# Hybrid decoder trunk on one core: the squares' round trip through memory moves from SyncE's to ScalarE's queue

## What is computed

```python
def _sqrelu_mlp(x, w1, w2):
    h = jax.nn.relu(x @ w1)      # w1: 2048 x 8192
    return (h * h) @ w2          # w2: 8192 x 2048
x = _layer_norm(DEEPNORM_ALPHA * x + y, ln_g[layer, 0], ln_b[layer, 0])
x = _layer_norm(DEEPNORM_ALPHA * x + _sqrelu_mlp(x, mlp_w1[layer], mlp_w2[layer]), ...)
```

## Time and profile before

| | |
|---|---|
| median of 3 runs | 2109.48 us |
| lowest, highest | 2108.84, 2110.66 us |
| the profiled execution | 2110.28 us |
| its span, first to last instruction | 2108.5 us |
| TensorE busy | 99% of the span |
| VectorE busy | 62% |
| ScalarE busy | 46% |
| memory traffic over the span | 208 GB/s |

### The profile page before, as it was taken

How to read it: one execution, slowest core, us unless ns; L and a number is a source line. 1 busy time by engine, 2 the same in 40 slices (tenths; PEclk the granted TensorE clock), 3 DMA queues, 4 the chain that set the end, 5 groups by cost and what they waited for, 6 DMA issues and landing times.

```text
span 2108.5 us, 28846 instructions
## 1 busy us (share of the span) xinstructions
PE 2091.5 (99%) x9914; PEld 1751.4 (83%) x9914; DVE 1316.9 (62%) x1246; ACT 975.1 (46%) x1140; POOL 21.3 (1%) x16
## 2 busy tenths in 40 slices
PE   9999999999999999999999999999999999999999
PEld 7898888888888888888988888888888888878887
DVE  5869666765655565565766666576755645555565
ACT  5596454443443443443644445354434434443442
POOL 0000010000000000000000000010000000000000
PEclk9999999999999999999999999999999999999999
DMA  7665757766766776675554556658766866766773
GB/s 243 190 204 187 238 180 250 248 201 197 242 219 184 242 229 195 204 253 166 190 187 161 164 169 228 201 191 255 233 199 203 256 198 190 250 198 225 241 229 100
DMA packets 249924, 439.68 MB, mean 209 GB/s; under 512 B 15056, under 2 KB 54224, under 8 KB 248816
## 3 DMA queue, kind: packets, MB, share of 16 engines
q1 hardware_dynamic: 248416, 432.79, 64.7%
q10 hardware_dynamic: 1424, 5.77, 0.7%
HBM read 419.63 MB, written 18.87 MB: 208 GB/s over the span
## 4 chain that ended last, share of the span: by engine, by line
PE 88%; DMA 4%; DVE 3%; issue 2%; ACT 2%; SPq 1%; ACTq 0%; DVEq 0%
PE ps L422 68%; PE ps L414 8%; PE ps L411 4%; DMA f<-sq_by_quad 2%; PE ps L707 1%; PE ps L706 1%; PE ps L705 1%; DMA sq_by_quad<-f 1%; DVE wl L992 1%; DVE gate L1066 1%; DMA wst<-in_rg_w_in_dram 1%; SPq L313 1%; ACT wh L738 1%; PE ps L552 1%; DVE f L1322 0%
## 5 line engine op out<-in xcount | busy, mean ns | idle before, releaser
L992 DVE TENSOR_TENSOR wl<-wst,wh 128x1024 fp32r<-128x1024 f32 x743 | 890.7, 1220 | 336.7 <-ACT wh L738 332.1
L738 ACT ACTIVATE wh<-wst 128x1024 fp32r<-128x1024 f32 x743 | 772.0, 1058 | 656.5 <-PE ps L422 416.1
L422 PE MATMUL ps<-wh,hid 128*128 128x512 f32 x2560 | 697.9, 390 | 5.9 <-DVE hid L1304 5.9
L422 PEld LDWEIGHTS ps<-wh,hid 128*128 128x128 f32 x2560 | 479.7, 188 | 107.9 <-issue 6.6
L422 PE MATMUL ps<-wh,xin 128*128 128x512 f32 x2048 | 548.9, 389 | 0.0
L422 PEld LDWEIGHTS ps<-wh,xin 128*128 128x128 f32 x2048 | 384.0, 188 | 79.3
L422 PE MATMUL ps<-wl,hid 128*128 128x512 f32 x1280 | 405.2, 390 | 0.0
L414 PE MATMUL ps<-xin,wh 128*128 128x512 f32 x960 | 332.4, 397 | 1.9 <-DVE wl L992 1.1
L422 PE MATMUL ps<-wl,xin 128*128 128x512 f32 x1024 | 315.2, 389 | 0.0
L422 PEld LDWEIGHTS ps<-wl,hid 128*128 128x128 f32 x1280 | 240.6, 188 | 50.2
L411 PE MATMUL ps<-xin,wl 128*128 128x256 f32 x960 | 257.3, 278 | 0.0
(11 more groups left out here) (138 smaller groups left out, 835.9 us busy)
## 6 DMA issues: line engine op xcount, KB each, us to landing
wst<-in_mlp_w_dram SPq DMA_DIRECT2D x512, 512.0 KB, 4.1
wst<-in_moba_w_qkv_dram SPq DMA_DIRECT2D x96, 512.0 KB, 4.6
wst<-in_rg_w_in_dram SPq DMA_DIRECT2D x62, 512.0 KB, 4.3
wst<-in_rg_w_out_dram SPq DMA_DIRECT2D x32, 512.0 KB, 4.7
sq_by_quad<-f SPq DMA_DIRECT2D x128, 128.0 KB, 2.9
f<-sq_by_quad SPq DMA_DIRECT2D x32, 512.0 KB, 5.1
wst<-in_moba_w_out_dram SPq DMA_DIRECT2D x32, 512.0 KB, 4.5
f<-in_x_dram SPq DMA_DIRECT2D x8, 256.0 KB, 6.3
```

The costliest lines, as they stand in the source:

```text
L422: return pe.matmul(banks(half)[:, a, :], src[:, c, part, a * P:(a + 1) * P], (wl if low else wh)[:, s, w], start=(c == 0 and part + low == 0),
L738: act.activation(wh[:, off % SPLITS, :], wst[:, slot, :], ACT.Copy).then_inc(wh_done, 1)
L992: dve.tensor_tensor(wl[:, off % SPLITS, :], wst[:, off % STAGE, :], wh[:, off % SPLITS, :], ALU.subtract).then_inc(wl_done, 1)
```

## The change

The two waits and the five DMAs of the squares' round trip go from SyncE's queue to ScalarE's, between the splits 14, 15 and 16. The relu is written in two instructions, one per 128 tokens, each in the order in which the scratch is laid out, so the DMAs out move pieces of 1 KB, and the transpose reads its input in order. The hidden channels come out in plain order, and W2 is loaded in plain order. The square multiplies `sqr` by itself. In the opening pair 1 is transposed before the first turn, and 5 warming matmuls stand first instead of 3.

```diff
-        sqr = f2[:, 0:1024].rearrange("p (a n) -> p a n", a=HALVES)
-        quad = f2[:, 1024:2048].rearrange("p (b n) -> p b n", n=P)
+        sqr = f2[:, 0:1024].rearrange("p (q n) -> p q n", q=GROUP)
+        quad = f2[:, 1024:2048].rearrange("p (i n) -> p i n", i=GROUP)
...
+        to_quad = by_quad.rearrange("(q t) (i n) -> i t q n", q=GROUP, i=GROUP)
...
-                to_quad = by_quad.rearrange("(q t) (a i n) -> i t a q n", q=GROUP, a=HALVES, n=P)
-
-                def squares_out(s, t):
-
-                    sp.wait_ge(psum_free, free + s * (2 * NG) + t + 1)
-                    for i in range(GROUP):
-                        sp.dma_start(to_quad[i], sqr[i * 32:(i + 1) * 32, :, :].rearrange("t a (q n) -> t a q n", n=P))\
-                          .then_inc(sq_out, 16)
-
-                def squares_back(s, t):
-                    sp.wait_ge(sq_out, (sq0 + s * NG + t + 1) * (16 * GROUP))
-                    sp.dma_start(quad, by_quad.rearrange("p (b n) -> p b n", n=P)).then_inc(sq_back, 16)
...
-                        src = w2[bass.ds(slab, 1), kb // 2 * COLS:(kb // 2 + 1) * COLS, bass.ds(col, COLS)]
-                        src = src.rearrange("s (p c) n -> p (s c) n", c=GROUP)
-                        load_block(src[:, kb % 2 * KCH:(kb % 2 + 1) * KCH, :], kb, b + kb)
+                        src = w2[bass.ds(slab, 1), kb * KCH * P:(kb + 1) * KCH * P, bass.ds(col, COLS)]
+                        load_block(src.rearrange("s (k p) n -> p (s k) n", p=P), kb, b + kb)
...
-            keep_warm(3)
+            keep_warm(5)
             input_pair(0)
             keep_warm(3)
+            input_pair(1)
             between = {k - 1: lambda k=k: input_pair(k) for k in range(2, BLOCKS)}
-            turn(xin, 0, B_U, R_X, {**between, BLOCKS - 1: parameters}, opening=lambda: input_pair(1))
+            turn(xin, 0, B_U, R_X, {**between, BLOCKS - 1: parameters}, halved=True)
...
-                        act.activation(sqr, banks(t % 2)[:, 0:HALVES, :], ACT.Relu).then_inc(sq_relu, 1)
-                        splits(b, no, LATE, NEXT)
+                        for a in range(HALVES):
+                            by_part = sqr.rearrange("p q (c a r) -> p a c q r", c=GROUP, a=HALVES)[:, a]
+                            by_col = banks(t % 2)[:, a, :].rearrange("p (c q r) -> p c q r", c=GROUP, q=GROUP)
+                            act.activation(by_part, by_col, ACT.Relu).then_inc(sq_relu, 1)
+                        splits(b, no, LATE, LATE + 1)
+                        act.wait_ge(psum_free, free + s * (2 * NG) + t + 1)
+                        for i in range(GROUP):
+                            act.dma_start(to_quad[i], sqr[i * 32:(i + 1) * 32, :, :]).then_inc(sq_out, 16)
+                        splits(b, no, LATE + 1, LATE + 2)
+                        act.wait_ge(sq_out, (sq + s * NG + t + 1) * (16 * GROUP))
+                        act.dma_start(quad, by_quad.rearrange("p (i n) -> p i n", i=GROUP)).then_inc(sq_back, 16)
+                        splits(b, no, LATE + 2, NEXT)
...
-                    dve.transpose(sq_t.rearrange("p c (b t) -> p b c t", t=32),
-                                  quad.rearrange("p b (r c) -> p b c r", c=GROUP)).then_inc(sq_turned, 1)
+                    dve.transpose(sq_t.rearrange("p c (a i t) -> p i (c a) t", a=HALVES, t=32),
+                                  quad.rearrange("p i (b r) -> p i b r", r=32)).then_inc(sq_turned, 1)
...
-                        dve.tensor_tensor(sqr, sqr, banks(t % 2)[:, 0:HALVES, :], ALU.mult).then_inc(psum_free, 1)
+                        dve.tensor_tensor(sqr, sqr, sqr, ALU.mult).then_inc(psum_free, 1)
```

More of the change, by code:

```diff
@@ L245, in load_block, with load_turn @@
                   .then_inc(stage_full[slot], 16)
-            def load_turn(w, col, b, also={}):
+            def load_turn(w, col, b):
                 col = sp.snap(col)
@@ L250, in load_turn @@
                 for kb in range(BLOCKS):
-                    if kb in also:
-                        also[kb]()
                     load_block(src[kb], kb, b + kb)
@@ L303, in load_rows, with load_mlp, load_w2 @@
                       .then_inc(rows_loaded, 16)
-            def load_mlp(layer, b0, sq0, free):
+            def load_mlp(layer, b0):
                 w2 = mlp_w2[layer].rearrange("(s r) n -> s r n", r=D)
-                to_quad = by_quad.rearrange("(q t) (a i n) -> i t a q n", q=GROUP, a=HALVES, n=P)
-                def squares_out(s, t):
-                    sp.wait_ge(psum_free, free + s * (2 * NG) + t + 1)
-                    for i in range(GROUP):
-                        sp.dma_start(to_quad[i], sqr[i * 32:(i + 1) * 32, :, :].rearrange("t a (q n) -> t a q n", n=P))\
-                          .then_inc(sq_out, 16)
-                def squares_back(s, t):
-                    sp.wait_ge(sq_out, (sq0 + s * NG + t + 1) * (16 * GROUP))
-                    sp.dma_start(quad, by_quad.rearrange("p (b n) -> p b n", n=P)).then_inc(sq_back, 16)
-                def load_w2(s, t, b, also={}):
+                def load_w2(s, t, b):
                     slab = sp.snap(s + 0)
@@ L323, in load_w2 @@
                     for kb in range(BLOCKS):
-                        if kb in also:
-                            also[kb]()
-                        src = w2[bass.ds(slab, 1), kb // 2 * COLS:(kb // 2 + 1) * COLS, bass.ds(col, COLS)]
-                        src = src.rearrange("s (p c) n -> p (s c) n", c=GROUP)
-                        load_block(src[:, kb % 2 * KCH:(kb % 2 + 1) * KCH, :], kb, b + kb)
+                        src = w2[bass.ds(slab, 1), kb * KCH * P:(kb + 1) * KCH * P, bass.ds(col, COLS)]
+                        load_block(src.rearrange("s (k p) n -> p (s k) n", p=P), kb, b + kb)
                 with sp.Fori(0, SLABS) as s:
-                    def squares(t):
-                        return {2: lambda: squares_out(s, t), 3: lambda: squares_back(s, t)}
-                    with sp.Fori(0, 2) as t:
+                    with sp.Fori(0, NG) as t:
                         load_turn(mlp_w1[layer], s * D + t * COLS, b0 + s * SLAB_BLOCKS + t * BLOCKS)
[L336 to L342, removed]
+                    with sp.Fori(0, NG) as t:
+                        load_w2(s, t, b0 + NG * BLOCKS + s * SLAB_BLOCKS + t * BLOCKS)
             load_rows(0)
-            load_mlp(0, B_MLP0, 0, T_MLP0)
+            load_mlp(0, B_MLP0)
             with sp.Fori(0, NG) as g:
@@ L352, in _ @@
                 load_turn(moba_w_out[0], t * COLS, B_MO + t * BLOCKS)
-            load_mlp(1, B_MLP1, SLABS * NG, T_MLP1)
+            load_mlp(1, B_MLP1)
             for h in range(HALVES):
@@ L388, in _, with turn @@
             by_twos = [(n, low) for m in range(0, GROUP, 2) for low in range(2) for n in (m, m + 1)]
-            def turn(src, half, b, ready, between={}, opening=None):
+            def turn(src, half, b, ready, between={}, halved=False):
                 dst = banks(half)
@@ L398, in turn @@
                     pe.wait_ge(pair_ready, ready + (kb + 1))
-                    if opening and kb == 0:
+                    if halved and kb == 0:
                         pe.wait_ge(first_lo, 1)
@@ L403, in turn @@
                     for c in range(kb * KCH, (kb + 1) * KCH):
-                        if opening and c == 1:
-                            opening()
+                        if halved and c == 1:
                             pe.wait_ge(wl_done, 1)
@@ L910, in out_unit, with mlp @@
                 last_pair(b0 + 2 * BLOCKS, b0 // BLOCKS + 2, n)
-            def mlp(b0, sq, n):
+            def mlp(b0, sq, free, n):
                 def squares_hi(s, t):
@@ L951, in _ @@
             out_unit(B_RO, 0)
-            mlp(B_MLP0, 0, 1)
+            mlp(B_MLP0, 0, T_MLP0, 1)
             with act.Fori(0, NG // 2) as it:
@@ L982, in _ @@
             out_unit(B_MO, 2)
-            mlp(B_MLP1, SLABS * NG, 3)
+            mlp(B_MLP1, SLABS * NG, T_MLP1, 3)
         @block.vector
@@ L1319, in w1_turns @@
                             splits(b, START, LATE)
-                        dve.wait_ge(sq_relu, sq + s * NG + t + 1)
-                        dve.tensor_tensor(sqr, sqr, banks(t % 2)[:, 0:HALVES, :], ALU.mult).then_inc(psum_free, 1)
+                        dve.wait_ge(sq_relu, (sq + s * NG + t + 1) * HALVES)
+                        dve.tensor_tensor(sqr, sqr, sqr, ALU.mult).then_inc(psum_free, 1)
                         splits(b, LATE, NEXT)
```

## The result

The changed kernel takes 2119.01 us (median of 20 runs, 2112.66 to 2124.47), the kernel before 2109.49 (20 runs, 2105.60 to 2116.34). The ratio is 1.0039, with a 95% interval of 1.0028 to 1.0049: slower by 0.4%, where 0.5% faster was forecast. The difference is small, but clear of the interval. The profiled execution took 2119.88 us, with a span of 2118.1; its rows stand against those of 2110.28.

The account below looks back on a forecast made before the run. TensorE was taken as the bound, stalling at eight W1-to-W2 crossings and in the opening. Gains of 8.8 us at crossings and 1.5 in the opening, 10.3 in all, gave 2099.6 us, with a range of 2096.7 to 2106.

Parts of the forecast that it names:

- What bounds the kernel, and how much is in it: TensorE, busy 99% of the span; its stalls at eight W1-to-W2 crossings cost 9.6 us, and the opening is second.
- all 9.6 and 3.2: Low end of the range: the whole crossing cost and the opening's far bound off the median, giving 2096.7 us.
- the four DMAs out: Squares' transfers to scratch at each round trip: landing forecast to change by -0.1 us (-0.3 to +1) on ScalarE's queue.
- The slower rival: DMA back beside weight blocks takes 6.3 us, transpose stays, crossings grow 0.8 to 1 us: 2119.5 us; chance 0.09.
- ScalarE's waits cost nothing: Splits 15 and 16 come about 2 us later behind ScalarE's new waits; its idle time was said to cover that.
- relu: Start of the squares' chain: two half instructions instead of one were to add 0.1 us (0 to +0.2).
- issues: Issuing the four DMAs out from ScalarE, 0.5 us apart, was to save 0.45 us per crossing (0 to -0.6).
- DMA back: Squares' return at a crossing, sharing engines with a weight block: -0.3 us (-1.0 to +1.2).
- transpose: Squares' transpose on VectorE, reading in order: from 1997 ns to near 1.2 us, -0.75 us (0 to -0.78).
- ScalarE's sequencer may not issue while a split runs: Rival "not what it says": the crossing's chain loses up to 0.5 us, landing in the partial case; no separate chance.
- The opening: Kernel start: weight block 1's first matmul at 13.2 instead of 14.70, -1.5 us (0 to -3.2).
- W2 in plain row order: Loading of W2: the same 2 KB pieces move, so nothing changes on the path.

Follow-up runs that it names:

- e9: e4 with SyncE's hold one block later, at block 18 (the block split 18 feeds): 2097.68 us, ratio 0.9940.
- e12: e4 with SyncE's hold at block 19 instead of block 17: 2113.85 us, ratio 1.0015.
- e5: e2 with ScalarE's wait for the DMAs out kept between splits 15 and 16, no DMA behind it: 2098.09 us, ratio 0.9941.
- e14: e12 with ScalarE's wait for the DMAs out and the DMA back moved behind split 16: 2112.04 us, ratio 1.0007.
- e4: The changed kernel, but SyncE starts block 17 only when the four DMAs out have landed: 2098.49 us, ratio 0.9949.
- e1: The kernel before with the opening part of the change alone: 2106.78 us, ratio 0.9991.
- e3: The kernel before with the opening and queue parts alone; relu, pieces, transpose and W2 in the old order: 2138.69 us, ratio 1.0134.
- e13: The changed kernel with ScalarE's wait for the DMAs out and the DMA back moved behind split 16: 2159.15 us, ratio 1.0235.
- e10: e2 with the DMA back moved ahead of block 18 on SyncE's queue, right behind the DMAs out: 2097.76 us, ratio 0.9940.
- e2: The changed kernel with the five DMAs and their waits back on SyncE's queue at their old places: 2102.01 us, ratio 0.9966.
- e7: e2 with the four DMAs out on ScalarE's queue, the wait and DMA back staying on SyncE's: 2097.95 us, ratio 0.9942.
- e8: e2 with the DMAs out and the DMA back each one block earlier on SyncE's queue: 2100.27 us, ratio 0.9950.
- e6: e2 with the wait and the DMA back on ScalarE's queue, the four DMAs out staying on SyncE's: 2105.05 us, ratio 0.9979.

## Why the prediction was wrong

*What bounds the kernel, and how much is in it:* right. The crossings and the opening account for what moved, and the floor of the experiments, 2097.7 to 2098.5, is 11.3 to 13.0 us below before in the same groups, against 12.8 for "all 9.6 and 3.2".

*The step that failed* is the one on the four DMAs out: "weight blocks no longer stand behind them in the same queue, they run beside: -0.1 (-0.3 to +1)". It took the running beside for harmless. It measured +1.3 by the page's medians and +3.0 for the last one at the crossings, thrice the bound. The prediction gives no row for that bound. Of the 32 last landings of before 30 are of 3.8 us or less: SyncE could not start block 18 before its fourth DMA out, nor block 19 before their landing. The longest stands at the first crossing, the one where block 17 started latest, 1.3 us after relu, so the effect could be seen in the trace of before:

```profile
399.66 5.17 DMA sq_by_quad<-f
```

I listed SyncE's waits as removed and called the blocks held "by the staging slots anyway". Block 18 moved from 5.2 to 3.7 us after relu, block 19 from 7.8 to 6.9, and the DMAs out needed until 9.0 us after relu, 9.9 at the crossings. The order in SyncE's program had been the protection, and the sum gave it no price. It could have been had from bytes: the four DMAs out, block 17 and block 18 are 1.5 MB, 4.1 us at the 383 GB/s that the trace of before shows between 8 and 11.8 us; with 2.3 us for a lone landing that is 8.8 us after relu when it starts at 2.4, and 9.0 was measured. This is an estimate made afterwards.

*The slower rival* had the mechanism and the wrong member of it: the DMA back got faster (5.0 to 4.2 at the crossings), the DMAs out slower. That its 2119.5 stands 0.5 us from the measured time is luck. It has the transpose at 2.0 and a crossing 0.8 to 1 us longer, where 1.35 was measured with the transpose 0.75 shorter; it has 15 us of stalls, three drops of the clock and 1.5 for the opening, where 17.5, two and 3.1 were measured. Its chance of 0.09 was far too low. The argument against it, that "no more blocks can be asked for than have a free staging slot", missed that one more is enough (e9 against e12).

*ScalarE's waits cost nothing:* right in e5 and e14, wrong in two places. In the first slab of each MLP VectorE has two steps of the residual between split 16 and the transpose. The timeline of the kernel after:

```profile
1498.05 0.35 ACTq L913 DMA_DIRECT2D f<-sq_by_quad  x1
1498.59 2.02 ACT L714 ACTIVATE wh<-wst 128x1024 fp32r<-128x1024 f32 x2 [6.00 <-DMA sq_by_quad<-f]
```

```profile
1499.68 1.23 DVE L978 TENSOR_TENSOR wl<-wst,wh 128x1024 fp32r<-128x1024 f32 x1 [5.84 <-ACT wh L714]
1500.83 1.22 DVE L1155 SCALAR_TENSOR_TENSOR f<-f,gate 128x1024 f32<-128x1024 f32 x1
1502.08 1.23 DVE L1160 SCALAR_TENSOR_TENSOR f<-gate,f 128x1024 f32<-128x1024 f32 x1
1503.22 1.24 DVE L1284 STREAM_TRANSPOSE f<-f 128x1024 f32<-128x1024 f32 x1
```

The squares were back 3.2 us after 1498.05, at 1501.2, and waited 2.0 us for this queue. Those two crossings hold the two longest stalls and both clock drops. I had followed the hold to the ring of weights and not to what stands between it and the transpose. So in the changed kernel the hold adds 1.5 and 2.0 us to these two trips. It does so only because the DMAs out land late: in e4, where they land early, it adds 1.0 us there and the low part is in time.

*The smaller terms:* relu +0.07 (said +0.1), issues -0.54 (-0.45), DMA back -0.8 (-0.3), transpose -0.75 (-0.75): all within their bounds. The Trainium skill (SBUF — State Buffer, Specifications (TRN2), the row on cachelines) says that each cross to a new 16-byte line pays a penalty. The transpose agrees: 1997 ns reading every fourth element, 1245 ns reading in order. *ScalarE's sequencer may not issue while a split runs* is wrong; it issued 0.2 us into one:

```profile
1845.38 1.06 ACT L714 ACTIVATE wh<-wst 128x1024 fp32r<-128x1024 f32 x1 [1.08 <-DMA wst<-in_mlp_w_dram]
1845.59 2.11 ACTq L910 DMA_DIRECT2D sq_by_quad<-f  x4
```

*The opening:* -3.1 instead of -1.5, near the far bound of -3.2; full pace came at 8.4 us and no longer at 11.4, so the weights alone decided: the low part of block 1 was done at 11.44, where 11.5 was forecast.

*W2 in plain row order* was put at nothing, and that is a second, smaller failure. In the last W2 turn of a slab, where no square is in flight, a block takes longer to land. The DMA views of that turn in the second slab, from 609.1 to 628.3 in the kernel before and from 609.7 to 628.9 in the kernel after:

```profile
wst<-in_mlp_w_dram SPq DMA_DIRECT2D x8, 512.0 KB, 3.6
...
wst<-in_mlp_w_dram SPq DMA_DIRECT2D x8, 512.0 KB, 4.5
```

It is so in every kernel here: 3.7 us with the old order (before, e1, e3), 4.6 to 4.7 with the new. At a crossing blocks 17 and 18 are W2's. In e13 (new order) and e3 (old order) block 17 starts 1.5 us after relu at the crossings and 1.5 and 1.1 at the second trip of a slab, where the blocks are still W1's. There the DMAs out have landed 8.5 us after relu in e13 and 9.5 in e3; at the crossings it is 11.1 and 9.8. This points to the slower W2 blocks for a part of the 3.0 us at the crossings. How much is open: no run moves the queue with the old order of W2 and the rest of the new form.

The Trainium skill (DMA: Bandwidth & Descriptors, "Issuing engines are not separate DMA queues") says that a second issuing engine saves only issue time. That it saves nothing in the transfers, the runs confirm: with no block started beside them the DMAs out land in 2.3 us from either queue (e9, e10). That moving a transfer can cost, through the blocks that are then free to start, e2 against the change shows: 2.6 us against 4.2 for the same 128 KB.

## What to carry to other kernels

A queue that carries both a prefetch stream and a short transfer that somebody waits for does more than issue: its waits keep the stream out of the engines while the short one is under way. Before a transfer moves to another queue, write down when each bulk block would start without those waits, and price the transfer with that block beside it; one block too many was worth 16 us here (e9 against e12). A wait that looks like a cost may be such a throttle, and taking it away may be what is slow (e13).

## What was not expected of the hardware

How far a short transfer is stretched. A DMA of 128 KB to memory, the last of four some 0.45 us apart, lands in 2.3 us when no load is started beside it (e4, e9), in 4.4 with one 512 KB load beside it on the other queue (the first trips of a slab in the change) and in 5 to 6 with two (its later trips). In the trace of the change the pieces of the four start over some 4 us (from 4.6 to 8.6 us after relu at the crossing of 1843), between those of the loads, where in e4 they start from 3.2 to 5.6. So it is the data that is late and not only the signal. The Trainium skill (DMA: Bandwidth & Descriptors, "Queues, rings and completion order") says that each DMA engine takes turns between its queues packet by packet. That fits the mixing of the pieces; how the turns are shared out was not tested.

A DMA of 512 KB from memory takes 3.3 us with nothing ahead (e7, e10), 4.1 with blocks started right behind it on the other queue (e4, e9), 5.2 to 5.6 behind one block in its own queue (e2, e8), and 5.7 beside two in flight (e6). And 512 KB of W2 in the same 2 KB pieces take 0.9 us longer when its rows are read in plain order; why, no run here tells.
